# A convolution stage on one core: five gate units at the end, and layer-norm sums with tokens on partitions

## What is computed

```python
h = rms_norm(x, norm_g)
a, b, z = jnp.split(h @ w_in, 3, axis=-1)
u = a * jax.nn.sigmoid(b)
u_ext = jnp.concatenate([prev, u], axis=1)
c = conv_general_dilated(u_ext, conv_w, depthwise, width 31) + conv_b
mu = mean(c, over the 2048 channels);  xc = c - mu
c = silu(xc * rsqrt(mean(xc * xc) + EPS) * ln_g + ln_b)
out = (c * jax.nn.silu(z)) @ w_out
```

## Time and profile before

| | |
|---|---|
| Median of three executions | 2427.46 us |
| Profiled execution, its own time | 2426.51 us |
| Its span, first to last instruction | 2424.7 us |
| Mean granted TensorE clock | 0.969 of full speed |
| Busy in the span | PE 2198.3, DVE 1314.0, POOL 1072.7, ACT 940.8 us |
| Instructions | 46974 |

### The profile page before, as it was taken

How to read it: one execution, slowest core, us unless ns; L and a number is a source line. 1 busy time by engine, 2 the same in 40 slices (tenths; PEclk the granted TensorE clock), 3 DMA queues, 4 the chain that set the end, 5 groups by cost and what they waited for, 6 DMA issues and landing times.

```text
span 2424.7 us, 46974 instructions
## 1 busy us (share of the span) xinstructions
PE 2198.3 (91%) x16540; PEld 1901.6 (78%) x16540; DVE 1314.0 (54%) x1892; ACT 940.8 (39%) x1617; POOL 1072.7 (44%) x715
## 2 busy tenths in 40 slices
PE   5999999999447997979999999988999998988999
PEld 3999999999337997978999888854555555558998
DVE  4698889889873004674787311113545444545332
ACT  4566556556452002231232112323454455453121
POOL 0688998898765112453324343222222222212230
PEclk7999999999789998999999999998999999999999
DMA  3222222222124112131412579999999999973212
GB/s 115 67 71 76 67 70 76 76 69 77 50 83 157 46 52 86 54 139 57 158 74 80 195 253 329 355 350 397 415 397 397 416 395 398 406 300 111 67 44 85
DMA packets 137487, 430.96 MB, mean 178 GB/s; under 512 B 23889, under 2 KB 40658, under 8 KB 136162
## 3 DMA queue, kind: packets, MB, share of 16 engines
q1 hardware_dynamic: 121554, 375.94, 41.8%
q0 software_dynamic: 13168, 41.58, 4.8%
q10 hardware_dynamic: 2592, 11.14, 1.1%
HBM read 386.81 MB, written 43.87 MB: 178 GB/s over the span
## 4 chain that ended last, share of the span: by engine, by line
PE 55%; POOL 15%; DVE 8%; issue 7%; ACT 6%; DMA 6%; SPq 2%; ACTq 0%; POOLq 0%; DVEq 0%
POOL ACC L1337 7%; PE PS L601 6%; PE PS L599 6%; PE PS L600 6%; PE PS L697 5%; PE PS L699 5%; PE PS L698 5%; PE PS L819 4%; PE PS L763 4%; DMA KV<-ck 2%; PE PS L898 2%; POOL ML L1367 2%; PE PS L607 2%; DMA KV<-cv 2%; PE PS L872 2%
## 5 line engine op out<-in xcount | busy, mean ns | idle before, releaser
L1310 POOL TENSOR_TENSOR WL<-RAW,WH 128x1024 fp32r<-128x1024 f32 (+1 forms) x121 | 306.2, 2531 | 583.6 <-ACT WH L948 579.0
L1650 DVE SCALAR_TENSOR_TENSOR PS<-UX,CWT,PS 128x1024 f32<-128x1024 f32 (+1 forms) x672 | 466.3, 786 | 0.0
L632 PE MATMUL PS<-HH,WH 128*128 128x384 f32 (+1 forms) x1152 | 378.4, 329 | 20.7 <-DVE HL L1636 20.7
L634 PE MATMUL PS<-HH,WL 128*128 128x384 f32 (+1 forms) x1152 | 377.4, 328 | 0.0
L633 PE MATMUL PS<-HL,WH 128*128 128x384 f32 (+1 forms) x1152 | 377.2, 327 | 0.0
L1337 POOL TENSOR_TENSOR ACC<-ACC,PROD 128x1088 f32<-128x1088 f32 x112 | 284.9, 2544 | 31.4 <-ACT PROD L1000 25.2
L697 PE MATMUL PS<-GH,WH 128*128 128x384 f32 (+1 forms) x792 | 266.8, 337 | 26.4 <-DVE KC L1762 12.1
L699 PE MATMUL PS<-GH,WL 128*128 128x384 f32 (+1 forms) x792 | 262.1, 331 | 0.0
L698 PE MATMUL PS<-GL,WH 128*128 128x384 f32 (+1 forms) x792 | 260.8, 329 | 0.0
L632 PEld LDWEIGHTS PS<-HH,WH 128*128 128x128 f32 x1152 | 217.3, 189 | 24.7 <-issue 13.7
L948 ACT ACTIVATE WH<-RAW 128x1024 fp32r<-128x1024 f32 (+1 forms) x121 | 131.4, 1087 | 252.7 <-PE PS L601 217.3
(11 more groups left out here) (213 smaller groups left out, 4318.7 us busy)
## 6 DMA issues: line engine op xcount, KB each, us to landing
KV<-ck SPq DMA_DIRECT2D x256, 512.0 KB, 11.3
KV<-cv SPq DMA_DIRECT2D x256, 512.0 KB, 11.8
RAW<-wA SPq DMA_DIRECT2D x48, 512.0 KB, 3.3
RAW<-wP SPq DMA_DIRECT2D x16, 640.0 KB, 3.9
zT_scr<-ZS ACTq DMA_DIRECT2D x16, 544.0 KB, 2.7
Z<-zT_scr SPq DMA_DIRECT2D x16, 544.0 KB, 3.6
RAW<-wB SPq DMA_DIRECT2D x17, 512.0 KB, 3.3
RAW<-wO SPq DMA_DIRECT2D x16, 512.0 KB, 3.3
```

What stands on the lines that cost most here:

```text
L632: pe.matmul(out, WH[w][:, kk], HH[:, k, a:b], start=k == 0, stop=False)
L634: mm = pe.matmul(out, WL[w][:, kk], HH[:, k, a:b], start=False, stop=k == KD - 1)
L1310: pool.tensor_tensor(WL[s][:, 0:n], RAW[s][:, 0:n], WH[s][:, 0:n].bitcast(F32), ALU.subtract).then_inc(s_lo, 1)
L1650: i = dve.scalar_tensor_tensor(out=o, in0=x, scalar=w[:, j:j + 1], in1=o, op0=ALU.mult, op1=ALU.add)
```

## The change

1. **Order of the units.** It is a list. Chunks 0, 4, 8, 12 and 15 have no z unit behind b and a; five z units (z11 to z15) come after a15. SP, PE, ACT and POOL follow the list and are written out without loops. Slots use four banks in turn (bank 4 is freed).
2. **Queue orders.** In a chunk without z, ACT has b of the next chunk where z was. POOL makes the next gate product ahead of a chunk's last addition. SP has all of a chunk's weight loads first and its twelve `past_logf` pages behind them. The loads of z for the layer norm wait for the square sums (`s_var` 10), since a buffer of theirs serves as a square tile.
3. **Sums.** POOL's CSUM is gone. PE sums a chunk over channels with the data as the stationary operand and one column of ones as the moving one, nine matmuls for nine blocks of tokens (`token_sums`), with tokens on partitions. The same is done for six pairs of squares and four single squares, with a ring of six tiles. The z14 and z15 slots stand between these.
4. **Root and reciprocal** work on nine columns (8 of 128 tokens and one of 64). PE spreads mean and reciprocal back to 128 x 1088 by nine matmuls (`spread`).

```diff
-        SLOT_BANK = ((0, 1, 2), (3, 4, 0), (1, 2, 3))
+        Z_WAITS = (0, 4, 8, 12, 15)
+        conv_order = []
+        for n in range(NCH):
+            conv_order += [(n, 0), (n, 1)]
+            if n not in Z_WAITS:
+                conv_order.append((n - sum(w < n for w in Z_WAITS), 2))
+        conv_order += [(n, 2) for n in range(NCH - len(Z_WAITS), NCH)]
+        place = {x: u for u, x in enumerate(conv_order)}
+        a_place = [place[n, 1] for n in range(NCH)]
+        TOK = [(c, min(P, R - P * c)) for c in range((R + P - 1) // P)]
...
-                for j in (5, 6, 7):
-                    u = 3 * n + j
...
-                            raw(u, at(wA, u), (s + j) % 2)
-                    past_logf(i, NPG // 2 * s + 4 * (j - 5), 4)
+                for u in range(a_place[n] + 4, a_place[n + 1] + 4 if n < NCH - 1 else U_OUT + 4):
+                    conv_raw(u)
+                for j in range(3):
+                    past_logf(n // 2, NPG // 2 * s + 4 * j, 4)
-            sp.wait_ge(s_zst, 16 * NCH)
-            sp.wait_ge(s_mmu, 1)
+            sp.wait_ge(s_var, 10)
             for n in range(NCH):
+                sp.wait_ge(s_zst, 16 * NCH)
                 atleast(sp, s_m, n - 1)
                 sp.dma_start(Z1[n % 2][:], zT[n]).then_inc(s_z1[n % 2], 16)
...
+            def token_sums(src, at, first, last):
+                for c, n in TOK[7:0:-1] + TOK[8:] + TOK[:1]:
+                    mm = pe.matmul(PS[0:n, 4, at + c:at + c + 1], src[:, P * c:P * c + n], ONES[:, 0:1],
+                                   start=first and c == 7, stop=last and c == 0)
+                return mm
+            def spread(src):
+                for c, n in TOK:
+                    mm = pe.matmul(CHAIN[:, P * c:P * c + n], src[0:n, c:c + 1].to_broadcast([n, P]), IDENT[0:n, 0:n],
+                                   start=True, stop=True)
+                return mm
+            for u, (n, kind) in enumerate(conv_order[:U_OUT - 2]):
+                conv_slots(u, range(3))
+                if kind == 1 and n >= 2:
+                    mean_sums(n - 2)
+                if u == a_place[NCH - 1] + 1:
+                    mean_sums(NCH - 2)
+            conv_slots(U_OUT - 2, (0,))
+            mean_sums(NCH - 1)
+            pe.wait_ge(s_mcp, 1)
+            spread(MST).then_inc(s_mmu, 1)
+            conv_slots(U_OUT - 2, (1, 2))
+            for r in range(3):
+                var_pair(r)
+                conv_slots(U_OUT - 1, (r,))
+            for p in range(3, 6):
+                var_pair(p)
+            for n in range(12, NCH):
+                pe.wait_ge(s_sq1, n + 1)
+                token_sums(SQ1[n % 6], VS, False, n == NCH - 1).then_inc(s_var, 1)
+            pe.wait_ge(s_vcp, 1)
+            spread(SDT).then_inc(s_rst, 1)
...
+            for n in range(NCH):                      # ACT
+                s, u = n % 2, a_place[n] + 1
+                three = n == NCH - 1 or a_place[n + 1] == u + 2
+                conv_hi(u + 1)
+                product(n, s, 0)
+                product(n, s, 1)
+                empty(u, 0)
                 product(n, s, 2)
+                empty(u, 1)
...
+            conv_hi(U_OUT)
+            for r in range(3):
+                for n in range(4 + 2 * r, 6 + 2 * r):
+                    square1(n)
+                empty(U_OUT - 1, r)
+            for n in range(10, 12):
+                square1(n)
+            conv_hi(U_OUT + 1)
...
+            for n in range(NCH):                      # POOL
+                s, u = n % 2, a_place[n] + 1
+                lo(u + 1, (u + 1) % 2)
                 adds(n, s, range(1, 3))
+                lo(u + 2, (u + 2) % 2)
                 adds(n, s, range(3, 6))
+                if n == NCH - 1 or a_place[n + 1] == u + 2:
+                    lo(u + 3, (u + 3) % 2)
+                adds(n, s, range(6, NT - 1))
+                if n < NCH - 1:
+                    gated(n + 1, 1 - s)
+                adds(n, s, range(NT - 1, NT))
+            lo(U_OUT - 1, (U_OUT - 1) % 2)
+            square_pair(0)
+            square_pair(1)
+            lo(U_OUT, U_OUT % 2)
+            for p in range(2, 6):
+                square_pair(p)
+            lo(U_OUT + 1, (U_OUT + 1) % 2)
...
-            dve.reciprocal(CHAIN, MU[:]).then_inc(s_inv, 1)
+            dve.reciprocal(SDT[:, 0:8], SDT[:, 0:8])
+            dve.reciprocal(SDT[0:RS, 8:9], SDT[0:RS, 8:9]).then_inc(s_vcp, 1)
```

More of the change, by code:

```diff
@@ L615, in _ @@
                 colsum(pe, 1, T0[k % 2], k == 0, k == KD - 1).then_inc(s_st0, 1)
[L617 to L635, removed]
@@ L637, in _, with conv_slots @@
-            paired(pe, NCH, chunk)
-            pe.wait_ge(s_csum, NCH + 1)
-            pe.wait_ge(s_eva, 9 * NCH)
[L640 to L646, removed]
+            def conv_slots(u, rs):
+                pe.wait_ge(s_lo, u + 1)
+                for r in rs:
+                    a, b = RCH[r]
+                    g = 3 * u + r
+                    atleast(pe, s_eva, g - 3)
+                    if g == 3:
+                        pe.wait_ge(s_sd0, 1)
+                    out = PS[:, slot_bank(g), 0:b - a]
+                    for k in range(KD):
+                        if g == 0:
+                            pe.wait_ge(s_h, k + 1)
+                        kk = slice(k * P, (k + 1) * P)
+                        pe.matmul(out, WH[u % 2][:, kk], HH[:, k, a:b], start=k == 0, stop=False)
+                        pe.matmul(out, WH[u % 2][:, kk], HL[:, k, a:b], start=False, stop=False)
+                        mm = pe.matmul(out, WL[u % 2][:, kk], HH[:, k, a:b], start=False, stop=k == KD - 1)
+                    mm.then_inc(s_slot, 1)
@@ L1008, in _, with square1 @@
                 copy_a(0, r)
[L1010 to L1014, removed]
+            def square1(n):
+                if n == 0:
+                    act.wait_ge(s_mmu, 1)
+                    act.wait_ge(s_cst, 32 * NCH)
+                act.wait_ge(s_xc, n + 1)
+                if n >= 6:
+                    act.wait_ge(s_var, n // 2 - 2)
+                act.activation(SQ1[n % 6][:], CC[:, n, :], ACT.Square).then_inc(s_sq1, 1)
@@ L1023, in chunk @@
-                act.dma_start(at(zT, n), ZS[:]).then_inc(s_zst, 16)
-                hi(3 * n + 4, hu[1], (s + 4) % 2, conv=True)
+                empty(u, 2)
+                conv_hi(u + 2)
                 product(n, s, 4)
[L1026 to L1055, removed]
+                if three:
+                    empty(u + 1, 0)
+                    product(n, s, 5)
+                    empty(u + 1, 1)
+                    product(n, s, 6)
+                    empty(u + 1, 2)
+                    conv_hi(u + 3)
+                    product(n, s, 7)
+                    empty(u + 2, 0)
+                    product(n, s, 8)
+                    empty(u + 2, 1)
+                    empty(u + 2, 2)
+                else:
+                    product(n, s, 5)
+                    product(n, s, 6)
+                    empty(u + 1, 0)
+                    product(n, s, 7)
+                    empty(u + 1, 1)
+                    empty(u + 1, 2)
+                    product(n, s, 8)
```

127 lines of the change are left out of this document (74 added, 53 removed).

## The result

| | before | after |
|---|---|---|
| median, us | 2426.97 (2426.24 to 2428.74, 4 runs) | 2458.88 (2457.87 to 2459.93, 4 runs) |
| profiled execution: time, span | 2426.51, 2424.7 | 2458.57, 2456.7 |
| mean granted clock | 0.969 | 0.958 |
| first low part ML | 698.18 | 731.12 |

The changed kernel is slower by 1.3%: ratio 1.0126, 95% interval 1.0114 to 1.0139. The forecast was 2447 within 2420 to 2463. ML starts 32.9 us later and the span is 32.0 us longer; the code behind ML gave back 0.9 at most.

A forecast was written before the change was run, and what follows sets the result against it. PE was taken to set the stage's pace, POOL's loop the rest; a15 at 609.7 - 47.4 + 24.7 + 16.8 + 0.8 + 4.5 = 609.1, plus 108.8, put ML at 717.9, +19.7 us: 2447 us, range 2420 to 2463.

The forecast's parts named there:

- 13 token sums: PE in the stage, ahead of a15: thirteen one-column sums at 1.9 us each, +24.7 us.
- PE's stands behind `cw`: Chunks 4, 8 and 12: PE stands 5.6 us each behind late cw, +16.8; chunk 0's low part +0.8.
- clock in the stage: PE's clock ahead of a15: 1.5 us lost behind each of three stalls, +4.5, between 0 and 9.
- T1 after a15: After PE's last sums, root, reciprocal and spread: T1 could start 91.9 us after a15.
- z issued: SP's queue at the end: loads of z issued only behind chunk 15's twelve pages, 102.5 us after a15.
- first ML after a15: POOL's first low part ML, set by z landing last: 108.8 us after a15, before 88.5.
- Part 2: Sums inside the stage on PE: priced by weight loads, 1.9 us each, thirteen ahead of a15, +24.7 us.
- Part 3: Waits for SP in the stage: twelve pages delay cw in chunks 4, 8 and 12, PE stands, +16.8 us.
- Part 4: The clock in the stage: falls behind three stalls of 5.6 us, 1.5 us each, +4.5, between 0 and 9.
- Part 5: From a15 to the first ML: 108.8 us against 88.5 before, z last, 11.7 us behind the rest.
- the forecast's sign: Trace sign at the end: DVE's product with z waits for a DMA after T1 has been idle some 10 us.
- Rival 3: SP's queue never decides, in the stage or at the end: -21.3 - 11.7, 2414 us, faster; chance 0.12.

The follow-up runs named there:

- e4: Changed kernel with the past_logf pages put between the weight loads in all chunks and no PE sums of chunks 0 to 14 (mean incomplete): 2406.61 us, ratio 0.9908.
- e1: Changed kernel with the past_logf pages put again behind each weight load in all chunks: 2434.94 us, ratio to before 1.0025.
- e10: Changed kernel with each token sum of the stage issued in three pieces, one behind each slot of its unit: 2458.43 us, ratio 1.0124.
- e2: Changed kernel with the past_logf pages mixed into the weight loads in chunk 15 only: 2460.23 us, ratio 1.0125.
- e5: e1 with two unused 384-column f32 matmuls ahead of each of PE's last seven sums of squares: 2431.18 us, ratio 1.0013.
- e9: Kernel before, with only the change's end: PE's eight square-pair sums with tokens on partitions, nine-column root and reciprocal, one spread: 2429.66 us, ratio 1.0001.
- e7: e1 with POOL adding chunks 0 to 14, PE summing that once, and all squares in pairs, eight sums: 2422.38 us, ratio 0.9971.

## Why the prediction was right, and where it missed

The direction and the range were right. The profiled execution came out 12.4 us above the 2446.2 of the sum. By its own steps:

| step | forecast, us | measured, us | shown by |
|---|---|---|---|
| four units less ahead of a15 | -47.4 | -46.8 | e4: a15 36.0 earlier, in spite of 7.4 of stands and 3.4 of clock |
| 13 token sums | +24.7 (1.9 each) | +26.0 (2.0 each) | PE's rows; e1 to e4 28.3 for 15 |
| PE's stands behind `cw` | +17.6 | +13.9 | waits; e1 |
| clock in the stage | +4.5 | +17.1 by stretches of 3 us | clock 0.97; e1, e10 |
| a15 | 609.1 | 619.6 | |
| c15 after a15 | 40.8 | 41.6 | |
| mean spread | 48.4 | 48.6 | |
| T1 after a15 | 91.9 | 106.2 | PE's rows at 0.50 |
| z issued | 102.5 | 105.4 | SP's queue |
| first ML after a15 | 108.8 | 111.5 | |

**Part 2 was right, and the figure that would have made it cheap is not for this case.** The two loads of 128 f32 columns set the price of a one-column matmul. The Trainium skill (TensorE: Matmul & The Clock Gate, "LDWEIGHTS (loading the stationary operand)") puts a load of 128 columns at 107 ns, which makes 1.8 us of 16 full and two half loads; the trace roughly agrees at 2.4 GHz, 2.0 us from one sum to the next, and at 1.2 GHz it was 3.8. The 25 ns of its section "Back-to-back issue gap" for 1 to 64 columns is there given for a matmul without the load, and the section itself says that it counts too little at few columns. Priced by it a sum would be 0.45 us, and e4 would have won a quarter of what it did.

**Part 3 was right**: chunks 4, 8 and 12, the page queue, the waits along the chain. The stands were 3.7 us too large in sum: 5.6 each in the forecast, 3.5, 5.0 and 3.3 in the trace, with 1.5 more at 380 behind a sigmoid that waits for `cw`. In e1, which takes the late landing away, the stands go and 24 us with them.

**Part 4 failed by size.** The step "for the three stalls of 5.6 us I take 1.5 each" counted only the falls behind the stands. Those cost 1.7, 3.4 and 1.7 us, 6.8 for the 4.5 forecast. The six falls behind token sums, 10.2 us, it had at nothing. The clock is 12.6 of the 13.2 us by which ML was later than forecast. The other terms, +0.6, +1.3, -3.7 and +2.7, nearly cancel, which is luck (the measured terms add up to 0.3 us too much). e10 shows that the sums bring their falls only in one piece, for none is left when they are split. e1 shows that with the stands three of these six go too. So in this kernel the clock's term is not one to be priced beside the stands alone. Why the same token sums let the clock fall half as often when PE never stands isn't settled by these runs.

**Part 5 came out near, but not by its own path.** It had T1 ready 11.7 us before z, so that a drop of the clock in the last seven sums would be worth nothing. The drop came, and T1 was 14.3 us later than "could start". Of these, 2.9 are the last pair of squares (POOL starts it at 698.91 and is done 81.8 us after a15, not 78.9). 9.6 are the five sums behind it (3.8 each, forecast 1.9), and 1.8 root, reciprocal and spread (5.2 for 3.5, with the spread at 4.4 for 2.4). z's issue was 2.9 late as well, behind the same late squares. So T1 and z came together, where the forecast's sign was a T1 idle for some 10 us: the slack held almost all of an error that was larger than it. That ML moved by only 2.7 is luck. e2 takes z's lateness away, and the half-clock sums are then as late.

Rival 3, SP's queue in time everywhere, was forecast at 2414; e1 is this case, at 2434.94. That rival left out the clock. By its terms a15 would be at 587.8, and e1 has it at 594.8: 5.1 us of clock, 1.3 for sums of 2.0 and 0.7 of stands. The first ML then comes 112.6 us after a15 and not 97.1. There the clock was 0.88 between 643 and 672, and six of the last seven sums ran at 3.8 us and the spread at 4.1; the filler of e5 gives back 3.8 of it.

## What to carry to other kernels

A queue that issues loads in order must be read as a resource with its own time per entry: moving twelve small issues behind the last load of a round cost 24 us with no byte moved differently. Before a sum is given to the engine that sets the pace, price it by its weight loads, and look whether another engine can take half of it; all of it on POOL made PE wait 16.9 us for low parts, half of it won. Runs of one-column matmuls went at half clock in the tails of these kernels, and so a short root and reciprocal bought with them gave nothing (e9).

## What the runs showed of the hardware

- Nine f32 matmuls of one column, 18 pairs of load and pass, take 2.14 us at 2.4 GHz and 3.94 at 1.2 GHz, so the time goes with the clock. In a row of such sums the last five of seven ran at 1.2 GHz in the changed kernel, six of seven in e1, the last ones in e7 and all eight in e9 (where PE came to them at 0.50 already), though PE counts as busy for nearly all of it (23.20 of 25 us in the changed kernel's 700 to 725).
- Six of the 13 token sums ahead of a15 in the changed kernel were followed by a fall of 1.7 us (three such falls in e1), and none in e10, where the same sums were issued in three pieces.
- Two matmuls of 384 columns ahead of each such sum held the clock at 0.99 in 655 to 690 of e5, where e1 without them has 0.70:

```profile
655.00:690.00 35.00, 35.00 (x232) 31.53 (x231) 6.45 (x6) 13.86 (x15) 11.88 (x5) 0.99 0.13 47
```

- Behind a stand of about 5 us the clock was at its lower level for some 6.8 us (e10), behind one of 3.5 us for about half as long (the changed kernel at 258 to 264).
